# adaLN modulation: the conditioning vectors become the stationary operand and the ada weights are streamed, 512 outputs at a time, in other places of the program

## The reference, cut to what matters

```
def ada_params(cond, w, b):
    m = jax.nn.silu(cond) @ w + b
    return [t[:, None, :] for t in jnp.split(m, 6, axis=-1)]
def modulate(h, shift, scale):
    return h * (1 + scale) + shift
...
    sh1, sc1, g1, sh2, sc2, g2 = ada_params(c, ada_w[i], ada_b[i])
    csh1, csc1, cg1, csh2, csc2, cg2 = ada_params(c_ctx[None, :], ada_w[i], ada_b[i])
    a_lat = modulate(rmsnorm(h_lat, mix_pre_g[i]), sh1, sc1)
    ...
    h_lat = h_lat + g1 * rmsnorm(m_lat, mix_post_g[i])
    f_lat = ffn(modulate(rmsnorm(h_lat, ffn_pre_g[i]), sh2, sc2))
    h_lat = h_lat + g2 * rmsnorm(f_lat, ffn_post_g[i])
```

## Time and profile before

| | us |
|---|---|
| median of 3 runs | 2714.45 |
| lowest, highest | 2705.26, 2714.47 |
| span of the profiled execution | 2699.9 |
| TensorE busy in it | 2432.5 |
| VectorE busy | 1322.1 |
| ScalarE busy | 1144.3 |

### The profile page before, as it was taken

How to read it: one execution, slowest core, us unless ns; L and a number is a source line. 1 busy time by engine, 2 the same in 40 slices (tenths; PEclk the granted TensorE clock), 3 DMA queues, 4 the chain that set the end, 5 groups by cost and what they waited for, 6 DMA issues and landing times.

```text
span 2699.9 us, 29721 instructions
## 1 busy us (share of the span) xinstructions
PE 2432.5 (90%) x10632; PEld 1840.9 (68%) x10633; DVE 1322.1 (49%) x1694; ACT 1144.3 (42%) x1436; POOL 36.1 (1%) x32
## 2 busy tenths in 40 slices
PE   4899977969999999688968999999999999999997
PEld 1455655538888888354657878787877777878785
DVE  1111045031111123315727878787964446878786
ACT  1201114141111112414435767676753335767675
POOL 0000013000000000000000000000000000000000
PEclk9998988878898889898979999999999999999999
DMA  6232300213333332210015979797964445979783
GB/s 225 94 125 94 125 0 1 82 43 121 120 132 124 125 125 94 90 63 1 12 54 207 359 281 363 269 366 272 362 229 156 164 163 189 359 280 357 295 344 138
DMA packets 68226, 472.56 MB, mean 175 GB/s; under 512 B 8119, under 2 KB 10328, under 8 KB 11544
## 3 DMA queue, kind: packets, MB, share of 16 engines
q1 hardware_dynamic: 64560, 463.50, 46.2%
q10 hardware_dynamic: 3560, 7.76, 0.8%
HBM read 470.18 MB, written 1.05 MB: 175 GB/s over the span
## 4 chain that ended last, share of the span: by engine, by line
PE 79%; DVE 9%; ACT 6%; issue 4%; ACTq 1%; DMA 1%; POOL 1%; DVEq 0%; POOLq 0%
PE bank L366 49%; PE bank L437 7%; PE bank L359 3%; PE bank L575 2%; PE bank L869 2%; DVE w_lo L1641 2%; PE bank L608 2%; ACT w_hi L1161 2%; PE bank L376 1%; PE bank L651 1%; PE bank L408 1%; PE bank L771 1%; PE bank L751 1%; PE bank L845 1%; DVE hT L1304 1%
## 5 line engine op out<-in xcount | busy, mean ns | idle before, releaser
L1641 DVE TENSOR_TENSOR w_lo<-ring,w_hi 128x1024 fp32r<-128x1024 f32 x672 | 797.4, 1222 | 208.1 <-ACT w_hi L1161 182.7
L1161 ACT ACTIVATE w_hi<-ring 128x1024 fp32r<-128x1024 f32 x672 | 697.7, 1059 | 266.0 <-PE bank L366 266.0
L366 PE MATMUL bank<-w_hi,x_hi 128*128 128x512 f32 x1008 | 409.6, 406 | 44.8 <-DVE x_lo L1682 24.3
L366 PE MATMUL bank<-w_hi,x_lo 128*128 128x512 f32 x1008 | 399.0, 396 | 0.0
L366 PE MATMUL bank<-w_lo,x_hi 128*128 128x512 f32 x1008 | 398.5, 395 | 0.0
L366 PEld LDWEIGHTS bank<-w_hi,x_hi 128*128 128x128 f32 x1008 | 193.3, 192 | 100.6 <-issue 43.3
L366 PEld LDWEIGHTS bank<-w_hi,x_lo 128*128 128x128 f32 x1008 | 192.8, 191 | 42.6
L366 PEld LDWEIGHTS bank<-w_lo,x_hi 128*128 128x128 f32 x1008 | 193.7, 192 | 38.4
L366 PE MATMUL bank<-w_hi,h_hi 128*128 128x512 f32 x504 | 196.9, 391 | 13.0 <-DVE h_lo L1655 13.0
L366 PE MATMUL bank<-w_hi,h_lo 128*128 128x512 f32 x504 | 196.7, 390 | 0.0
L366 PE MATMUL bank<-w_lo,h_hi 128*128 128x512 f32 x504 | 196.1, 389 | 0.0
(11 more groups left out here) (283 smaller groups left out, 2957.1 us busy)
## 6 DMA issues: line engine op xcount, KB each, us to landing
ring<-in_moe SPq DMA_DIRECT2D x336, 1024.0 KB, 5.5
ring<-in_pre SPq DMA_DIRECT2D x105, 1024.0 KB, 4.8
hT<-in_xT ACTq DMA_DIRECT2D x1, 2048.0 KB
out_T<-hT SPq DMA_DIRECT2D x2, 512.0 KB, 2.9
arena<-in_q_up ACTq DMA_DIRECT2D x1, 768.0 KB, 5.3
arena<-in_w_krv ACTq DMA_DIRECT2D x1, 640.0 KB, 3.8
mT<-in_decay ACTq DMA_DIRECT2D x1, 512.0 KB
arena<-in_dft ACTq DMA_DIRECT2D x1, 512.0 KB
```

What stands on the lines that cost most here:

```text
L366: m = pe.matmul(out, x[a], w[b], start=(first and n == 0), stop=(last and n == 2))
L1161: act.activation(w_hi[:, h % 4, :], ring[:, s % SLOTS, (h % 2) * UNIT:(h % 2 + 1) * UNIT], ACT.Copy).then_inc(sem("w_high"), 1)
L1641: dve.tensor_tensor(w_lo[:, h % 4, :], ring[:, (N_PRE + n) % SLOTS, (h % 2) * UNIT:(h % 2 + 1) * UNIT], w_hi[:, h % 4, :].bitcast(F32), AL ...
```

## The change

Now all 48 ada slots are in one form. Two slots hold one group of 512 outputs: each slot has four of the eight contraction tiles, and each tile moves 512 columns of weights past a stationary 128 x 32 matrix `cond32`, whose columns beyond the first two are zero (`ada_half`). All eight tiles of a group accumulate into the same 32 partitions of one bank. ScalarE copies these 32 rows into SBUF (`ada_copy`, `ffn_rows`), and four ordinary matmuls against two columns of the identity turn them into columns (`ada_columns`). A layer has 12 groups.

The groups stand in other places. Groups 0 to 3 stay at the start. Groups 4 to 11, whose weights went with EVIN and EVOUT, now run in the eight passes of the SSD loop, one in each, behind the `rows` of the next pass. Group 12 stands between the two norm sums behind EVOUT. Groups 13 to 23 run in the FFN, one behind each pair of gate/up slots. The order of the slots in `pre` follows.

In the FFN the split parts have two buffers (`fw2_hi` and `fw2_lo` lie over `aT`), so that ScalarE and VectorE work one gate/up slot ahead.

```
+            def ada_half(g, half, dst):
+                for j in range(4):
+                    m = pe.matmul(dst[0:32, :], cond32[:, 4 * half + j, :],
+                                  ring[:, (ada_slot(g) + half) % SLOTS, j * 512:(j + 1) * 512],
+                                  start=(half == 0 and j == 0), stop=(half == 1 and j == 3))
                 m.then_inc(sem("slot_used"), 1)
+            def ada_group(g, dst):
+                if g >= 2:
+                    pe.wait_ge(sem("ada_rows"), g - 1)
+                for half in range(2):
+                    slot_wait(ada_slot(g) + half)
+                    ada_half(g, half, dst)
+            def ada_columns(g, i=None):
+                for t in range(4):
+                    at = 8 * (g % ADA_G) + 2 * t
+                    cols = slice(at, at + 2) if i is None else bass.ds(i * 24 + at, 2)
+                    m = pe.matmul(bank[6][:, cols], ada_rows(g)[0:32, t * P:(t + 1) * P], ident[0:32, 0:2], start=True, stop=True)
+                m.then_inc(sem("ada_turned"), 1)
...
@@ EVIN
-                n = S_EVIN + 2 * s
+                n = S_EVIN + s
-                ada_slot(n + 1, bank[6], 2 * s)
@@ SSD loop
                     rows(r + 2)
                     rows(r + 3)
+                ada_group(G_EVIN + r // 2, bank[2 + r // 2 % 2])
+                if r:
+                    ada_turn(G_EVIN + r // 2 - 1)
                 pe.wait_ge(sem("sc_ready"), r + 2)
@@ EVOUT
-                ada_slot(n + 1, bank[6], 2 * (N_EVIN + s))
             norm_sum(POST0, lambda k: aT[:, k, :])
+            ada_group(ADA_G, ada_bank(ADA_G))
             norm_sum(FPRE0, lambda k: aT[:, k, :])
@@ FFN, TensorE
+            def gate_up_pair(m, i=None):
+                e = 0 if i is None else i
+                pe.wait_ge(sem("hff_done"), e * 6 + (2 * m + 1))
+                gate_up(0, e * 12 + 4 * m)
+                pe.wait_ge(sem("ada_rows"), e * 3 + (ADA_G + m + 1))
+                ada_columns(G_FFN + m - 1, i)
+                pe.wait_ge(sem("hff_done"), e * 6 + (2 * m + 2))
+                gate_up(1, e * 12 + (4 * m + 2))
+                g = G_FFN + m
+                for half in range(2):
...
+                    ada_half(g, half, ada_bank(g))
@@ SSD loop, ScalarE
+                if r >= 2 and r % 2 == 0:
+                    ada_copy(G_EVIN + r // 2 - 1, bank[2 + (r // 2 - 1) % 2])
+            ada_copy(ADA_G - 1, bank[3])
@@ FFN, ScalarE
-                act.wait_ge(sem("slot_used"), used + (s - 1))
+                if q >= 2:
+                    act.wait_ge(sem("slot_used"), used + (gu_slot(q - 2) + 1))
...
+                for q in range(2, 8):
+                    if q % 2 == 0:
+                        ffn_rows(G_FFN + q // 2 - 1, i * 12, i * 3)
+                    ffn_silu(q, i * 12, i * 6)
+                    ffn_high(q + 2, i * 12, i * 32)
@@ VectorE, behind the FFN
-            dve.wait_ge(sem("slot_used"), S_DOWN)
+            dve.wait_ge(sem("ada_turned"), 2 * ADA_G)
```

More of the change, by code:

```diff
@@ L52 @@
 N_ODOUT = 4
[L53 to L57, removed]
+S_EVIN = 2 * G_EVIN
+S_ADAB = S_EVIN + N_EVIN
+S_EVOUT = S_ADAB + 2 * (ADA_G - G_EVIN)
+S_ADAC = S_EVOUT + N_EVOUT
+S_GU = S_ADAC + 2
+S_DOWN = S_GU + 2 * NFF
 S_ODIN = S_DOWN + N_DOWN
@@ L110, in gate_slot, with gu_slot, ada_slot @@
     return 0 if g == 0 else 6 * g - 2
+def gu_slot(q):
+    return S_GU + 4 * (q // 2) + q % 2
+def ada_slot(g):
+    if g < G_EVIN:
+        return 2 * g
+    if g < ADA_G:
+        return S_ADAB + 2 * (g - G_EVIN)
+    if g < G_FFN:
+        return S_ADAC
+    return S_GU + 4 * (g - G_FFN) + 2
 def down_slot(g):
@@ L392, in _ @@
             pe.wait_ge(sem("cond_ready"), 1)
[L394 to L413, removed]
+            for g in range(G_EVIN):
+                ada_group(g, bank[g % 2])
+                if g:
+                    ada_turn(g - 1)
+            ada_turn(G_EVIN - 1)
             norm_sum(PRE0, lambda k: aT[:, k, :])
@@ L597, in _ @@
             GR = NFF // 6
             with pe.Fori(0, GR) as i:
[L599 to L617, removed]
+                for m in range(3):
+                    gate_up_pair(m, i)
+            for m in range(3 * GR, NFF // 2):
+                gate_up_pair(m)
+            ada_turn(2 * ADA_G - 1)
@@ L1061, in ffn_tile, with ffn_rows @@
                 act.activation(sg[:, q % 2, :], bank[2 * (q % 2)][:, :], ACT.Silu).then_inc(sem("sg_ready"), 1)
-            with act.Fori(0, NFF // 6) as i:
-                for q in range(6):
-                    ffn_tile(q, i * 12, i * 32, i * 6)
-            for q in range(NFF // 6 * 6, NFF):
-                ffn_tile(q, 0, 0, 0)
+            def ffn_rows(g, used, turned):
+                act.wait_ge(sem("slot_used"), used + (ada_slot(g) + 2))
+                act.wait_ge(sem("ada_turned"), turned + (g - 1))
+                act.activation(ada_rows(g)[0:32, :], ada_bank(g)[0:32, :], ACT.Copy).then_inc(sem("ada_rows"), 1)
@@ new lines, in _ @@
+            ffn_high(0, 0, 0)
+            act.wait_ge(sem("fx_split"), KD)
+            ffn_high(1, 0, 0)
+            for q in range(2):
+                ffn_silu(q, 0, 0)
+                ffn_high(q + 2, 0, 0)
+            with act.Fori(0, NFF // 6) as i:
+                for q in range(2, 8):
[3 more added lines that the diff above has]
+                    ffn_high(q + 2, i * 12, i * 32)
@@ L1068, in _ @@
+            for q in range(NFF // 6 * 6 + 2, NFF):
+                if q % 2 == 0:
+                    ffn_rows(G_FFN + q // 2 - 1, 0, 0)
+                ffn_silu(q, 0, 0)
+            ffn_rows(2 * ADA_G - 1, 0, 0)
             for f in range(NFF):
@@ L1864, in layout @@
     evin = units(np.concatenate([ev[:, 0:1536], ev[:, 2048:3072], ev[:, 1536:2048]], 1), 24)
-    ada = [units(f("ada_w")[l], 48) for l in range(2)]
+    ada = np.concatenate([f("ada_w")[l].reshape(2, 4, P, ADA_G, 512).transpose(3, 0, 2, 1, 4) for l in range(2)], 0)
+    ada = ada.reshape(2 * ADA_G, 2, P, 2, UNIT)
     evout = units(f("ev_w_out")[0], 8)
@@ L1878, in layout @@
     pair = lambda x, s: [x[2 * s], x[2 * s + 1]]
-    for s in range(N_ADA_A):
-        slots.append(pair(ada[0], s))
-    for s in range(N_EVIN):
-        slots += [pair(evin, s), pair(ada[0], N_ADA_A + s)]
-    for s in range(N_EVOUT):
-        slots += [pair(evout, s), pair(ada[0], N_ADA_A + N_EVIN + s)]
-    for j in range(NFF):
-        slots += [[gate[j], up[j]], pair(ada[1], j)]
-    for s in range(N_ADA_C):
-        slots.append(pair(ada[1], NFF + s))
+    ada_pair = lambda g: [(ada[g, h, :, 0], ada[g, h, :, 1]) for h in range(2)]
+    for g in range(G_EVIN):
+        slots += ada_pair(g)
+    slots += [pair(evin, s) for s in range(N_EVIN)]
+    for g in range(G_EVIN, ADA_G):
+        slots += ada_pair(g)
+    slots += [pair(evout, s) for s in range(N_EVOUT)]
+    slots += ada_pair(ADA_G)
+    for m in range(NFF // 2):
+        slots += [[gate[2 * m], up[2 * m]], [gate[2 * m + 1], up[2 * m + 1]]] + ada_pair(G_FFN + m)
     slots += [pair(down, s) for s in range(N_DOWN)]
```

109 lines of the change are left out of this document (63 added, 46 removed).

## The result

The changed kernel takes **2613.0 us** (median of 4 runs, 2611.86 to 2615.14), the kernel before 2709.9 in the runs taken beside it (4 runs, 2703.33 to 2714.47). The ratio is 0.9646, 95% interval 0.9627 to 0.9666.

A forecast was written before the change was run, and what follows sets the result against it. TensorE was taken as the bound, by its work and clock. Terms -56.7 + 50.0 - 27.4 - 38.7 + 2.2 = -70.6 took 2714.45 to 2644 us, range 2626 to 2670.

The forecast's parts named there:

- the terms: Stage changes summed: EVIN -56.7, SSD loop +50.0, EVOUT with norm sum -27.4, FFN -38.7, start +2.2 us.
- The clock mechanism: Across EVIN, EVOUT and FFN: narrow matmuls precede clock falls, streaming keeps 2.4 GHz; about 52 of the 70 us.
- The price of 3.46 a slot: Each streamed ada slot on TensorE: 8 instructions at 0.4325 us, 3.46 us, nothing saved against the former 3.47.
- my 91.1: SSD loop with eight ada groups: 91.1 us after, against 41.2 before, +50.0.
- Rival (C): EVIN, EVOUT, FFN: the clock doesn't recover, FFN rhythm or pauses bring the falls; 52 us come back, 2696; chance 0.07.
- rival (D): Ada groups: 32-column matmuls count as little work, so the clock falls inside them; 70 us over (C), 2766; chance 0.04.
- rival (E): SSD loop: passes wait for ScalarE's copy of a group, 7 us more, 2651; chance 0.07.
- rival (B): TensorE around groups and turnings: a drain at each change of shape, 62 x 0.18 = 11 us, 2655; chance 0.17.
- One reading in the prediction: EVIN's clock windows: an ada slot's two-column matmuls end a stretch at clock 1.00; the next stretch is at 0.55.
- The experts' part must not change: Expert stage: no change expected; if it did change, the sum would be of another kernel than thought.
- with the same distance the time is 2714.45 - 70.6: Whole kernel: the median stays 14.55 us above the profiled span, as before, giving 2644 us.
- the terms for what lies ahead of the down projection: All stages from the start through the FFN: together -70.6 us, with no term for L446's 16-column matmuls.

The follow-up runs named there:

- Experiment 4: The changed kernel with the four contraction tiles of a slot sent to four column groups, the turning adding the four parts: 2498.5 us, ratio 0.922 to the kernel before.
- Experiments 5 and 6: Empty activations around ScalarE's expert loop: kernel before, 17 ahead, 2687.76 us; changed kernel, 47, 110 or 111 ahead, 2662.6, 2652.65, 2660.7 us, 110 behind, 2615.4 us.
- experiment 1: The changed kernel with all groups computed by narrow two-column matmuls at the new places, without row copies and turnings: 2727.88 us, ratio 1.0073 to the kernel before.
- Experiment 7: The kernel before, unchanged, profiled once more: span 2702.3 us, its own time 2704.14 us.
- 110 ahead: The changed kernel with 110 one-column activations on ScalarE beside the down projection, ahead of the expert loop: 2652.65 us.
- experiment 2: The kernel before with its 40 narrow ada slots streamed at their old places, most modulation sums left out: 2517.55 us, whole time not comparable.

## Why the prediction was wrong

**Right: the terms.** EVIN, the SSD loop, EVOUT and the FFN came within 0.8, 0.3, 1.3 and 1.8 us. The clock mechanism holds in both directions: streamed slots at the old places bring EVIN to 13.93 a slot, narrow ones at the new places bring the clock to 0.50 inside a group. The price of 3.46 a slot held (6.98 for two), and so did the passes of the SSD loop; my 91.1 is 91.5 in the trace. Rival (C) and rival (D) are ruled out by the clock of 1.00 in the groups and 11.1 to 11.4 in the slots, rival (E) by rows that begin where the products end and by a turning that begins where the group ends. Of rival (B), for which I drew on the Trainium skill, TensorEngine Tiling (Array Packing), section Key Properties, at most 4 us came on top of the sum instead of 11. Experiment 4 fits a price of some 0.15 us a change, most of which the terms taken from the trace held already; these runs don't tell a drain from another small cost.

One reading in the prediction is off, without weight for the sum: the ada slot doesn't stand at the end of the stretch from 170.20 to 173.60. It runs from 169.21 to 172.68 and fills the first 2.5 us, so the clock falls some 1 us behind its end:

```profile
169.21 3.47 PE bank L359 x32
```

**Wrong, first step: "The experts' part must not change."** It gave 13.2 us. No term of the sum stood for it, because the diff has nothing there. But the edit moved the code of ScalarE's expert loop, and waits at its turns, which nothing in the profile released, went away. Experiments 5 and 6 show the cause as far as the place of the code; 17 instructions saved 16 us, and 110 cost 40. Why the place matters stays open. The sign of the 13.2 was luck: the kernel of experiment 1, which has most of the same edits, kept its 53 packets and 1262.5 us of experts.

**Wrong, second step: "with the same distance the time is 2714.45 - 70.6".** The profiled span and the median are 14.55 apart, of which 1.8 is what lies around every span; the other 12.7 is that the profiled execution was a short one of a kernel whose times spread over 24 us, and that the median of three was a high one (the 12 and 13 later runs have 2706.8 and 2703.6). Experiment 7 shows what goes with the spread: the clock falls come at other slots each time, and the longest runs have the lowest mean clock. The changed kernel has few falls left; its four runs lie within 3.3 us and its median 1.1 above its profiled run. The kernel of experiment 4 and the one with 110 ahead, four runs each, spread over 10 and 13 us, so the change has not made every kernel like it steady. I had carried the distance over as a constant. Against the span, with 1.8 around it, my sum gives 2631.1.

**Mis-sized:** the terms for what lies ahead of the down projection, 76.6 instead of 70.6. L446, now L481, took 8.86 instead of 12.40. Windows over it, in the kernel after:

```profile
269.87:273.00 3.13, 3.13 (x31) 3.13 (x30) 0.00 (x0) 0.60 (x1) 0.00 (x0) 1.00 0.62 178
273.00:276.00 3.00, 3.00 (x24) 3.00 (x24) 0.00 (x0) 0.00 (x0) 0.00 (x0) 0.80 0.39 164
276.00:278.73 2.73, 2.73 (x14) 2.73 (x15) 0.00 (x0) 0.00 (x0) 0.00 (x0) 0.50 0.02 6
```

The clock falls here too, from 1.00 to 0.50, but later. Before, an ada slot stood ahead of it, and the clock was at 0.67 already in its first stretch, and at 0.50 at 333.6:

```profile
326.25:330.00 3.75, 3.75 (x25) 3.75 (x25) 0.00 (x0) 0.00 (x0) 0.00 (x0) 0.67 0.92 312
```

I had named this line as one that comes ahead of falls, and not asked at which clock it would start. The start and the residual give 2.3 more and the way to EVOUT 0.2; the errors of the four large terms cancel.

The account: 2631.1 - 6.0 - 13.2 = 2611.9, the time of the profiled run. Of the 31 us between 2644 and 2613, then, some 12 are the carried distance, 6 the terms ahead of the down projection and 13 the experts.

## What to carry to other kernels

A profiled execution of a kernel with clock falls is one draw: sum against its span plus what lies around it, and ask whether the change also removes what makes the runs differ. Before costing a narrow or streamed form by its own duration, look at what the work behind it takes. When a control gives the expected total, check that the time went in the stage that was edited. And a loop whose turns show waits that nothing released deserves a control with a few empty instructions ahead of it; here that was worth as much as a middling edit, and an A/B of two kernels should be read with it in mind.

## What the runs showed of the hardware

- With more or less code ahead of ScalarE's expert loop, the experts' part took 1242 to 1252 us with 18 or 19 instruction packets on the queue, and 1262 to 1297 with 53 or 54; no profiled execution had a number in between (experiment 2, with other rows in the experts, is left out).
- 16 matmul instructions of 128 x 32 by 512 columns in four column groups take 1.85 us; in one group 6.98.
- 64 instructions of two-column matmuls on end take 9 to 11 us at a clock that falls to 0.50 inside them; 32 of them took 3.47 at the full one.
- At the start of the narrow kernel 256 such instructions took 54.70 us, 0.21 each, while the windows give a clock of 1.00. Later 0.19 goes with 0.50. The norm sum behind them, of 512-column matmuls, took 10.01 us at a recorded 1.00 instead of the 7.06 of the changed kernel. Two forms slow in the same stretch speak for a record of the clock that doesn't hold at the start; no run settles it:

```profile
60.00:75.00 15.00, 15.00 (x72) 15.00 (x72) 0.00 (x0) 0.00 (x0) 0.00 (x0) 1.00 0.47 163
...
102.00:110.00 8.00, 8.00 (x13) 3.17 (x12) 0.09 (x1) 0.00 (x0) 0.00 (x0) 1.00 0.62 240
```
